# Last layer of a fused two-block network: gates projected last and turned, the attention's division moved into the gates, output and store by tile

## The reference

```python
def odd_layer(h_lat, h_ctx, w_in, sink, w_out, rope, ctx_out):
    q, k, v, g = split_cols(h_lat @ w_in, ODD_SPLITS)
    ...
    y_l = (windowed_gqa(q, k, v, ck, cv, sink_hg) * jax.nn.silu(g)) @ w_out
```

## Time and profile before

| | us |
|---|---|
| median of 3 runs (1219.1 to 1223.7) | 1220.16 |
| the profiled execution | 1221.05 |
| its span from first to last instruction | 1219.2 |
| PE busy | 1121.4 (92%) |
| DVE busy | 723.7 (59%) |
| ACT busy | 583.4 (48%) |
| POOL busy | 125.8 (10%) |
| mean granted clock of PE | 0.967 |

### The profile page before, as it was taken

One profiled execution on the slowest core, in us unless ns is written; L12 is line 12 of the kernel. 1 busy time (PEld: TensorE's weight loads), 2 busy tenths in 40 slices (PEclk: granted clock), 3 DMA queues, 4 the chain that ended last, 5 costly groups with the idle time before them and its releaser, 6 DMA issues.

```text
span 1219.2 us, 15226 instructions
## 1 busy us (share of the span) xinstructions
PE 1121.4 (92%) x5781; PEld 915.2 (75%) x5781; DVE 723.7 (59%) x1186; ACT 583.4 (48%) x1069; POOL 125.8 (10%) x121
## 2 busy tenths in 40 slices
PE   4998899999999997899999998999989797996996
PEld 4997577888887995768888866897867686885765
DVE  4858766666546868666666446233553525468783
ACT  4543555565436543565564344243356414254762
POOL 1405010000001442010000000001000012012002
PEclk9999899999999998999999998999999897998999
DMA  8552568666557543676656674233110022250000
GB/s 299 167 155 88 173 184 283 182 182 189 183 165 277 170 121 122 203 232 203 187 179 186 189 253 141 69 94 104 46 60 1 36 71 84 70 190 17 1 1 35
DMA packets 109378, 170.43 MB, mean 140 GB/s; under 512 B 7293, under 2 KB 72826, under 8 KB 109050
## 3 DMA queue, kind: packets, MB, share of 16 engines
q1 hardware_dynamic: 108170, 164.42, 43.2%
q0 software_dynamic: 992, 3.67, 0.8%
q10 hardware_dynamic: 144, 1.38, 0.3%
HBM read 168.39 MB, written 1.05 MB: 139 GB/s over the span
## 4 chain that ended last, share of the span: by engine, by line
PE 79%; DVE 13%; ACT 4%; issue 2%; DMA 1%; POOL 1%; DVEq 0%; SPq 0%; POOLq 0%; ACTq 0%
PE PS L454 17%; PE PS L455 17%; PE PS L456 17%; DVE low L430 5%; PE PS L2363 3%; PE PS L2361 3%; PE PS L2362 3%; PE PS L1456 2%; PE PS L1474 2%; PE PS L1464 1%; PE PS L1513 1%; PE PS L663 1%; PE PS L1284 1%; PE PS L867 1%; DMA raw<-w_mod 1%
## 5 line engine op out<-in xcount | busy, mean ns | idle before, releaser
L454 PE MATMUL PS<-high,hT_high 128*128 128x512 f32 (+3 forms) x908 | 350.6, 386 | 16.4 <-DVE low L430 6.6
L455 PE MATMUL PS<-low,hT_high 128*128 128x512 f32 (+3 forms) x908 | 345.5, 380 | 0.0
L456 PE MATMUL PS<-high,hT_low 128*128 128x512 f32 (+3 forms) x908 | 344.8, 380 | 0.0
L430 DVE SCALAR_TENSOR_TENSOR low<-raw,vec_cols,high 128x512 fp32r<-128x512 f32 (+1 forms) x304 | 232.2, 810 | 107.4 <-ACT high L420 107.3
L427 DVE TENSOR_TENSOR low<-raw,high 128x1024 fp32r<-128x1024 f32 (+2 forms) x122 | 144.6, 1192 | 198.6 <-ACT high L417 198.5
L420 ACT ACTIVATE high<-raw,vec_cols 128x512 fp32r<-128x512 f32 (+1 forms) x304 | 190.1, 675 | 114.8 <-PE PS L456 112.8
L417 ACT ACTIVATE high<-raw 128x1024 fp32r<-128x1024 f32 (+2 forms) x122 | 124.8, 1030 | 201.5 <-PE PS L456 139.3
L454 PEld LDWEIGHTS PS<-high,hT_high 128*128 128x128 f32 x908 | 172.8, 190 | 50.3 <-DVE low L430 14.7
L456 PEld LDWEIGHTS PS<-high,hT_low 128*128 128x128 f32 x908 | 172.7, 190 | 27.9
L455 PEld LDWEIGHTS PS<-low,hT_high 128*128 128x128 f32 x908 | 172.7, 190 | 25.8
L2361 PE MATMUL PS<-high,fT_high 128*128 128x512 f32 x176 | 69.8, 396 | 0.0
(11 more groups left out here) (315 smaller groups left out, 1454.9 us busy)
## 6 DMA issues: line engine op xcount, KB each, us to landing
raw<-w_gate_up SPq DMA_DIRECT2D x176, 256.0 KB
raw<-w_in SPq DMA_DIRECT2D x64, 400.0 KB
raw<-w_mod SPq DMA_DIRECT2D x48, 512.0 KB
raw<-w_down SPq DMA_DIRECT2D x44, 512.0 KB
raw<-o_w_in SPq DMA_DIRECT2D x20, 512.0 KB
raw<-w_out SPq DMA_DIRECT2D x16, 512.0 KB
raw<-e_w_in SPq DMA_DIRECT2D x12, 512.0 KB
raw<-e_w_out SPq DMA_DIRECT2D x8, 512.0 KB
```

Source lines behind the costliest of these rows:

```text
L430: last = e.scalar_tensor_tensor(g.low[:, i, :], g.raw[:, i, :], g.gain[:, i:i + 1], g.high[:, i, :].bitcast(F32), ALU.mult, ALU.subtract)
L454: e.matmul(bank, xh[:, k, tokens], g.high[:, i, :], start=first and i == 0, stop=False)
L455: e.matmul(bank, xh[:, k, tokens], g.low[:, i, :], start=False, stop=False)
L456: done = e.matmul(bank, xl[:, k, tokens], g.high[:, i, :], start=False, stop=last and i == len(g.rows) - 1)
```

## The change

Three things change in the last layer, and nothing before its first chunk is taken.

1. *Order and form of the projection.* The chunks come as kv, q0, q1, g0, g1. The keys are turned behind q0, each half of the queries is turned behind the next chunk. The gates' products have their operands changed over (`turned_products`): 128 weight columns are stationary and the 256 tokens move, so that the result comes out turned. Tanh (ACT) and g * (1 + tanh) (DVE) read PSUM. The queries get a place of their own (`o_q`).
2. *Division.* The weights are turned unscaled, one step behind the scores. The sums of a group of eight steps (four heads) are inverted together, `gqa_spread_pe` spreads them over the partitions by eight products with the identity, and DVE multiplies the gates by them, and then by the attention's result. The sink's logits are made for a group at once. DVE copies every fourth block of turned weights. The output's first four weight granules are cut inside the attention. The window's product has 128 columns.
3. *Output.* The first four granules cover the features of the first half for both column halves, the last four the rest, tile 0 ahead of tile 1. DVE adds to x, ACT squares by 512 columns, the root and the store go by tile and by half.

```diff
@@ o_in, o_out
-            ("kv", O_K), ("g0", O_G), ("g1", O_G + 512), ("q0", 0), ("q1", 512))]
+            ("kv", O_K), ("q0", 0), ("q1", 512), ("g0", O_G), ("g1", O_G + 512))]
+        for j, rows in OUT_ORDER:
+            o_out.add(a["o_w_out_2"][0], rows, 512 * j, 512).half = j
@@ new
+        def turned_products(e, ph, xT, banks, free):
...
+            for g in ph.granules:
+                low_ready(e, g)
+                for b in range(4):
...
+                    for i, k in enumerate(g.rows):
+                        e.matmul(bank, g.high[:, i, cols], xh[:, k, :], start=k == 0 and b % 2 == 0, stop=False)
+                        e.matmul(bank, g.high[:, i, cols], xl[:, k, :], start=False, stop=False)
+                        done = e.matmul(bank, g.low[:, i, cols], xh[:, k, :], start=False,
+                                        stop=k == DK - 1 and b % 2 == 1)
@@ new
+        def gqa_spread_pe(e, g):
+            e.wait_ge(dve.sem, dve.value(f"gqa_inverse{g}"))
+            if g >= 2:
+                e.wait_ge(dve.sem, dve.value(f"yo_F{g - 2}"))
+            for i in range(GROUP_STEPS * g, GROUP_STEPS * (g + 1)):
+                h, t, _ = gqa_steps[i]
+                last = e.matmul(gqa_out(spread_bank(g), h, t), e_den[:, i:i + 1].broadcast_to([P, HD]), ident,
+                                start=True, stop=True)
@@ gqa_attention_pe (in place of attention_pe for this layer)
+            for i in range(n + 3):
+                if i < n:
...
+                if 1 <= i < n + 1:
+                    j = i - 1
+                    e.wait_ge(act.sem, act.value(f"gqa_exp{j}"))
...
+                j = i - 2
+                if j >= 1:
...
+                    if j == n - 1:
+                        gqa_spread_pe(e, GROUPS - 1)
...
+                    if j % GROUP_STEPS == 2 and 2 < j < n:
+                        gqa_spread_pe(e, j // GROUP_STEPS - 1)
@@ gqa_attention_act
+                if i >= 1 and (i - 1) % 4 != 3:
+                    gqa_copy(e, act, i - 1)
...
+                if i in (17, 21, 25, 29):
+                    cuts.to(o_out.granules[(i - 17) // 4])
@@ gqa_scores
+            far = SEQ + (1 - t) * P
+            mul(bank[:, far:far + P], ident_high[:, :], window_high[:, t, :], start=False, stop=False)
@@ gates
+        def gates_silu_dve(e, cuts, c):
+            ph = o_in[3 + c]
+            cuts.to(ph.last, 3 if c == 0 else 0)
+            for t in range(2):
+                e.wait_ge(act.sem, act.value(f"g_tanh{c}{t}"))
+                e.scalar_tensor_tensor(gT[:, 4 * c + 2 * t:4 * c + 2 * t + 2, :].rearrange("p k s -> p (k s)"),
+                                       q_in[:, t, 512 * c:512 * (c + 1)], 1.0, PS[:, O_BANKS[3 + c][t], :],
+                                       ALU.add, ALU.mult).then_inc(dve.sem, dve.mark(f"gT{2 * c + t}"))
+            if c == 0:
+                cuts.to(o_in[4].last)
@@ late_dve, behind the attention
+            for t in range(NT):
+                for j in range(2):
...
+                    e.tensor_tensor(gated[:, 2 * t + j, :], PS[:, O_OUT_BANKS[t][j], :], post_gain[:, 0, cols],
...
+                    e.tensor_tensor(x[:, t, cols], x[:, t, cols], gated[:, 2 * t + j, :],
...
@@ late_pe
-            q_turn_pe(e)
+            q_turn_pe(e, 0)
+            turned_products(e, o_in[3], hT, O_BANKS[3], lambda b: taken(e, "o_in_q0", b))
+            q_turn_pe(e, 1)
+            turned_products(e, o_in[4], hT, O_BANKS[4], lambda b: e.wait_ge(dve.sem, dve.value(f"q_low{2 + b}")))
             e.wait_ge(dve.sem, dve.value("q_low7"))
+            gqa_attention_pe(e)
```

More of the change, by code:

```diff
@@ new lines, in late_act @@
+            gates_tanh_act(e, cuts, 0)
+            for i in range(4, 8):
+                gqa_high_act(e, i)
+            gates_tanh_act(e, cuts, 1)
+            gqa_attention_act(e, cuts)
+            cuts.to(o_out.last)
+            for t in range(NT):
+                for j in range(2):
+                    e.wait_ge(dve.sem, dve.value(f"final_x{t}{j}"))
+                    e.activation(xn[:, t, j * 512:(j + 1) * 512], x[:, t, j * 512:(j + 1) * 512], ACT.Square, scale=1 / 32,
+                                 accum_out=final_parts[:, 2 * t + j:2 * t + j + 1]).then_inc(act.sem, act.mark(f"final_squares{t}{j}"))
@@ new lines, in late_pe @@
+            for t in range(NT):
+                for g in o_out.granules[4:8]:
+                    if t == 0:
+                        low_ready(e, g)
+                        ready(g.rows[0], 0)
+                    done = products(e, g, t, hT, PS[:, O_OUT_BANKS[t][g.half], :], False, g.rows[-1] == DK - 1)
+                    if t == 1:
+                        done.then_inc(granules_done, 1)
+                    elif g.rows[-1] == DK - 1:
+                        done.then_inc(pe.sem, pe.mark(f"o_out_product{g.half}"))
```

366 lines of the change are left out of this document (229 added, 137 removed).

## The result

The changed kernel takes 1210.13 us (median, 1206.41 to 1212.69) where the kernel before took 1221.93 beside it (median, 1219.10 to 1229.49). The medians are 11.8 us apart; the ratio estimated from the same runs is 0.9875, 95% interval 0.9843 to 0.9907, which is 11.4 to 19.2 us. 1210.0 (1206.5 to 1215.5) was predicted. The profiled execution took 1211.59 us, span 1209.8.

The account below looks back on a forecast made before the run. TensorE was taken as the attention's bound, but only just. Front -12.0, attention +4.3, output and store -2.6 sum to -10.3: 1221.05 becomes 1210.75, and with the median 0.9 lower, 1210.0 us is predicted, range 1206.5 to 1215.5.

Parts of the forecast that it names:

- Front, -12.0: Last layer's projection up to the first scores: reordered chunks and no gate transposes start the scores 12.0 us earlier.
- Attention, +4.3: First scores to first output product: division removed, but spreads, gating and weight cuts added, 4.3 us longer in sum.
- Start +1.5: Attention's beginning: last silu delays the first maximum 0.8 us, transposes precede the third scores, 0.5, plus settling; +1.5 us.
- Spreads +3.5: Eight spread products per group on TensorE at 1.2 us, three groups inside the steps, less what is absorbed: +3.5 us.
- Late help +2.2: Last 16 attention steps: four weight cuts at 0.4 us each and gating delaying three maxima by 0.2; +2.2 us.
- End -0.6: Last scores to first output product: 7.2 us instead of 7.8, with all gating in line; -0.6 us.
- Period, -2.3: Attention steps: a pair takes 3.73 us by the scores-exponential-transposes chain instead of 3.89, over 15 pairs; -2.3 us.
- Window product, 0: Attention scores: shrinking it from 256 to 128 columns gains 0, since the load behind takes its 0.12 us anyway.
- Tail, -2.6: Last output product to the end: finishing by tile and half saves 2.2 us, the smaller store perhaps 0.4; -2.6 us.
- The loads: Rival, 7%: weight loads come into line in the turned chunks; +10.6 us at 0.172 per product, total 1220.6.
- The attention takes more back: Rival, 12%: ACT's and DVE's inserted work all on the path, spreads one by one; attention 7.6 us longer, 1217.6.
- Better: Rival, 6%: window's 1.9 us, half the start's and late help's costs, and the store's 1.3 gained; about 1206 us.

Follow-up runs that it names:

- lag2: Changed kernel with transposes two steps behind the scores, values three, VectorE's copy moved along: 1213.35 us, ratio 0.9917 to the kernel before.
- combined: lag2b_start plus twelve output products issued inside the attention's end, four weight cuts moved to early steps, third group's columns made later: 1208.20 us, ratio 0.9848 to before.
- combined2: combined with VectorE's gating split over two neighbouring steps, group parts and cuts in own steps, six output products one place earlier: 1207.51 us, ratio 0.9846 to before.
- lag2b_start: lag2 with gating one step later, its low part two, and the last gates' second silu half behind the first maximum: 1210.14 us, ratio 0.9892 to before.
- lag2b_start_pool: lag2b_start with the low parts of the output's first four weight granules cut by GpSimd instead of VectorE: 1214.25 us, ratio 0.9926 to before.

## Why the prediction was right

The steps of the sum were right in kind and the total within 0.6 us by stretches, with two sizes off and one effect missing, as follows. That the median, 1210.13, meets 1210.0 to 0.1 us is luck: the same kernel gave 1213.60 in its second set.

- **Front, -12.0.** Measured -12.17. The turned products cost what I had taken from the 288-wide stream, the upper end did not come up. The tightest cover was where I had put it:

```profile
1086.96 0.88 DVE L770 TENSOR_TENSOR xn<-z_late,consts 128x256 f32<-128x256 f32 x1
...
1093.60 2.52 DVE L1867 SCALAR_TENSOR_TENSOR o_q<-PS,o_q 64x512 fp32r<-64x512 f32 x4
1096.14 3.50 DVE L433 TENSOR_TENSOR low<-raw,high 128x1024 fp32r<-128x1024 f32 x3
```

VectorE's second rotation (1086.96 to 1093.5, 6.5 us instead of 5.74, with GpSimd's beside it) left its first cut for g1 to end at 1096.14 + 3.50 / 3 = 1097.3, and TensorE came for it at 1098.1. Of 1.5 us of slack some 0.8 were left.
- **Attention, +4.3.** Measured +4.05, with terms that were off in both directions. Start +1.5: it was +2.4 (+2.1 when run again); the waits were priced, the lower clock after them was not, and how the 2.4 divides between the two is open. Spreads +3.5: +2.6. Late help +2.2: cuts 1.3 and gating 2 x 0.18, 1.7; the third gating falls behind the last scores. End -0.6: -1.0.
- **Period, -2.3**, the term that was mis-sized: 52.97 + 2.62 + 1.31 + 0.36 = 57.26 would be the old steps with what was added, 55.61 was measured, so -1.65 (and 15 x 0.16 is 2.4, not 2.3). Of that 0.63 is the first of these steps (1.81 for 2.44), and the 13 pairs behind it gave 0.07 to 0.08 each, not 0.16. In the rows above, scores to transposes are 2.65 us (1129.13 to 1131.78) for the 2.61 of the prediction, and transposes to the next scores but one 1.17 (to 1132.95) for 1.12: together 3.82 for 3.73. lag2 shows that this chain was the bound: with the transposes one step later the pairs are 3.60.
- **Window product, 0; output 22.5.** Both numbers as stated, and both tested; the reason for the 0 was wrong (a product after 0.06, not 0.12, and the gain lost again behind it).
- **Tail, -2.6.** -2.8 in the profile, -2.9 by undoing it.
- **The sum.** -12.17 + 4.05 - 2.8 = -10.9 by stretches, for -10.3. The medians differ by 11.8, and the interval of the ratio is 11.4 to 19.2 us, which just leaves 10.9 out; the repeated run's interval (0.73 to 1.29%, 8.9 to 15.8 us) holds 10.9. The difference can lie ahead of the change, in the part that varies by 10 us from one execution to the next; the profiles don't show more than that.
- **The rivals.** The loads did not come into line, tested by all 192 turned products. "The attention takes more back" needed cuts of 1.03 us each on the path and spreads at 1.72; they cost 0.33 and 0.87. "Better" would have needed 4 us; the start gave nothing of it, the window nothing, the late help 0.5 and the tail 0.2 to 0.3.
- **The signs.** Of those set down, two did not come: the clock at 2.4 GHz throughout (0.80 over the first four steps), and pairs of 3.7 (3.82). The three places of +1.2 were +0.87.

What I did not see: that the kernel before had made the output's first four cuts under its last projection. The term "late help" counted them as work that the new attention does besides; the experiment with the old attention shows that they are the price of the new front. What was not tried:

```profile
1108.17 0.60 ACT L1784 ACTIVATE z_late<-PS 128x512 f32<-128x512 f32 x1 [8.06 <-PE PS L517]
1108.87 0.69 DVE L1795 SCALAR_TENSOR_TENSOR z_late<-z_late,PS 128x512 f32<-128x512 f32 x1 [4.02 <-ACT z_late L1784]
```

ScalarE stands idle for 8.06 us ahead of the tanh of the last gates and VectorE for 4.02 ahead of its silu, while g1's granules come free one by one, as q1's did before. Three of the four cuts might go there; whether they would, stays open. What is shown is a cheaper place for them than the one chosen: in the early steps of the attention, with the transposes two steps behind (combined), they cost nothing. With the transposes one step behind that was not tried.

## To carry to other kernels

When a chunk of work is moved into a gap, list what else the gap held: here it held the next phase's weight cuts, and they cost 1.3 us in the late steps of the attention, 4.7 behind it, and nothing in its early steps once the transposes ran two steps behind. Split a stretch of many equal steps into its period, its exceptions and its two ends, and price each by itself; the sum came out right here by errors of both signs, and only the parts told where 6 us more could be had. An engine between two that hand work to each other has slack per step, not per stretch: here VectorE's gating of 1.4 us in one step cost 0.5 (combined), and divided between two steps it cost no more than 0.1 (combined2).

## What the runs showed of the hardware

- TensorE's granted clock over the attention's first four steps was 0.75 to 0.80 in all nine profiles in which TensorE's longest wait there was 1.84 to 2.04 us, and 1.00 in the five with 1.21 (lag2b_start and its three descendants) or 1.45 (before). Nothing between was measured there. The length of one wait does not decide it: in the end of lag2b_start the clock fell behind a wait of 1.83 us, but in lag2b_start_pool it fell to 0.50 behind waits of only 0.51 and 1.03 us in neighbouring steps, where lag2b_start kept 1.00 behind one of 1.20.
- While GpSimd subtracted 128x1024 elements in SBUF (2.37 us), the VectorE operation on 128x1 elements of SBUF started beside it ended only with it (0.16 us became up to 1.96), while VectorE's maximum from PSUM beside it kept its 0.69.
- The 256-column products with a load each ran 0.117 us apart. The 128-column ones in the scores were followed after 0.06, and there nothing was won: 0.05 of the 0.06 came back in the next gap.
